# Attention on one Trainium2 core: PSUM shared out with four banks for scores and three in the ring of turned blocks

## The reference, cut to what matters

```python
s = jnp.einsum('bqgre,bige->bqgri', qg, kc) * SCALE          # scores
p_cmp, _ = _masked_softmax(s, mask)                          # mask, exp(s - max), divide by the sum
o_cmp = jnp.einsum('bqgri,bige->bqgre', p_cmp, vc)           # probabilities times values
...
o = g[..., 0:1] * o_cmp + g[..., 1:2] * o_slc + g[..., 2:3] * o_win
```

## Time and profile before

| | us |
|---|---|
| median of 3 runs | 1948.7 |
| lowest and highest run | 1945.65 and 1949.38 |
| profiled execution, its time | 1947.66 |
| profiled execution, its span | 1945.5 |
| TensorE busy in the span | 1826.0 (94%) |
| VectorE, ScalarE, GpSimd busy | 1041.1, 755.8, 264.0 |

### The profile page before, as it was taken

The page is one execution under the profiler, slowest core; times in us unless marked ns, Lnnn a source line. Parts: engine busy times, 40 slices in busy tenths (PEclk is TensorE's granted clock), DMA queues, the critical chain, the costliest instruction groups (busy, mean ns, idle before and its releaser), DMA issues. The chain is left out here.

```text
span 1945.5 us, 31487 instructions
## 1 busy us (share of the span) xinstructions
PE 1826.0 (94%) x12115; PEld 1539.0 (79%) x12115; DVE 1041.1 (54%) x2536; ACT 755.8 (39%) x1583; POOL 264.0 (14%) x344
## 2 busy tenths in 40 slices
PE   5999998988999889999987999999999999999998
PEld 4777787886777666666656889989989989989987
DVE  5978835335666566666654444344444444444444
ACT  4544433205777556655543233222212212213211
POOL 1000000003444344444430000000000000000000
PEclk8999999998999999999998999999999999999999
DMA  5233233515666322232236221212213113112202
GB/s 187 89 111 130 106 118 105 167 25 136 180 172 165 91 92 89 90 116 85 86 92 201 76 79 61 92 65 74 78 66 107 46 66 108 44 65 92 82 22 97
DMA packets 172107, 192.30 MB, mean 99 GB/s; under 512 B 55334, under 2 KB 138534, under 8 KB 169688
## 3 DMA queue, kind: packets, MB, share of 16 engines
q1 hardware_dynamic: 169618, 175.70, 28.9%
q0 software_dynamic: 2352, 14.73, 2.2%
HBM read 168.72 MB, written 59.81 MB: 117 GB/s over the span
## 5 line engine op out<-in xcount | busy, mean ns | idle before, releaser
L2274 PE MATMUL o_py<-f_h_hi,m_gu_hi 128*128 128x384 f32 (+1 forms) x1056 | 196.7, 328 | 0.5 <-DVE m_gu_lo L2458 0.5
L2274 PE MATMUL o_py<-f_h_lo,m_gu_hi 128*128 128x384 f32 (+1 forms) x1056 | 195.3, 327 | 0.0
L2274 PE MATMUL o_py<-f_h_hi,m_gu_lo 128*128 128x384 f32 (+1 forms) x1056 | 195.3, 327 | 0.0
L1847 DVE CUSTOM_DVE_ANT_0 l_e<-l_s,k_masks 128x1024 f32<-128x1024 f32 (+3 forms) x192 | 138.4, 721 | 103.9 <-PE l_s L1492 101.2
L2274 PEld LDWEIGHTS o_py<-f_h_hi,m_gu_hi 128*128 128x128 f32 x1056 | 176.8, 188 | 10.8 <-issue 8.1
L1792 ACT ACTIVATE l_e<-l_e,l_nmin 128x640 f32<-128x640 f32 (+11 forms) x224 | 169.0, 754 | 33.8 <-DVE l_nmin L1847 32.0
L2274 PEld LDWEIGHTS o_py<-f_h_lo,m_gu_hi 128*128 128x128 f32 x1056 | 176.9, 188 | 0.0
L2274 PEld LDWEIGHTS o_py<-f_h_hi,m_gu_lo 128*128 128x128 f32 x1056 | 176.9, 188 | 0.0
L2509 DVE SCALAR_TENSOR_TENSOR a_kv_nat<-m_ext,m_taps,a_kv_nat 128x384 f32<-128x384 f32 (+1 forms) x66 | 37.9, 574 | 170.5 <-ACT m_ext L2397 157.4
L2396 ACT ACTIVATE a_kv_nat<-o_py,m_taps 128x384 f32<-128x384 f32 (+1 forms) x33 | 21.6, 655 | 272.8 <-PE o_py L2274 272.8
L1532 PE MATMUL l_t<-k_ident,l_e 128*128 128x128 f32 x816 | 123.6, 276 | 0.2 <-DVE l_pT L1844 0.2
(11 more groups left out here) (305 smaller groups left out, 3642.5 us busy)
## 6 DMA issues: line engine op xcount, KB each, us to landing
m_raw_gu<-in_w_gate SPq DMA_DIRECT2D x22, 512.0 KB, 4.0
m_raw_gu<-in_w_up SPq DMA_DIRECT2D x22, 512.0 KB, 5.3
m_raw_d<-in_w_down SPq DMA_DIRECT2D x11, 1024.0 KB, 4.8
k_first<-in_w_in SPq DMA_DIRECT2D x5, 2048.0 KB, 8.2
a_kd_k<-in_state_dil SPq DMA_DIRECT2D x8, 1024.0 KB, 8.2
a_kd_v<-in_state_dil SPq DMA_DIRECT2D x8, 1024.0 KB, 7.9
a_kd_k<-in_cache_slc SPq DMA_DIRECT2D x128, 64.0 KB, 1.9
k_w<-in_w POOLq DMA_DIRECT2D x4, 1024.0 KB, 6.4
```

The source lines that it names most:

```text
L1847: return nc.vector.tensor_tensor_reduce(out=dst, in0=src, in1=m, scale=1.0, scalar=CLAMP, op0=ALU.add, op1=ALU.min, accum_out=low)
L2274: last = nc.tensor.matmul(bank[q % 2][:, 0:w], ws[k][:, m, c, :], hs[:, c, t0:t0 + w], start=(j == 0 and c == 0), stop=(j == 2 and c == KC ...
```

## The change

The number of score banks becomes a constant of four and the ring has three banks instead of four. The output bank stays. `score_banks` places every unit anew by the same rule over four banks.

```diff
-    used, at, prior = [-1, -1, -1], {}, {}
+    used, at, prior = [-1] * S_BANKS, {}, {}
     for u in range(NU):
         n = -(-width(u) // 512)
-        first = min(range(3 - n + 1), key=lambda x: (max(used[x:x + n]), x))
+        first = min(range(S_BANKS - n + 1), key=lambda x: (max(used[x:x + n]), x))
...
-RING = 4
+RING = 3
+S_BANKS = 4
...
-        s_all = ctx.enter_context(nc.psum_tensor("l_s", [P, 3 * 512], F32))
+        s_all = ctx.enter_context(nc.psum_tensor("l_s", [P, S_BANKS * 512], F32))
         S_AT, S_PRIOR = score_banks()
-        s_ps = lambda u: s_all[:, S_AT[u] * 512:min(S_AT[u] * 512 + 1024, 3 * 512)]
+        s_ps = lambda u: s_all[:, S_AT[u] * 512:min(S_AT[u] * 512 + 1024, S_BANKS * 512)]
```

## The result

The changed kernel takes 1951.8 us (median of 20 runs) against 1948.6 for the kernel before (median of 20): ratio 1.0018, 95% interval 1.0011 to 1.0024. It is 3.2 us slower. The direction was forecast and the time lies in the range, but the sum was +8.6 us, so more than half of it did not come. The profiled execution has a span of 1950.8 us, 5.3 more than that of before. Of these 1.3 us lie ahead of the attention part and some 1.1 behind it, where the change touches nothing; the attention part itself is 2.8 us longer.

What follows compares the result with a forecast made beforehand. TensorE was taken as the full engine: busy 189.0 of 198 us in the dilated passes, 339.6 of 379 in the sparse. 14.8 + 7.0 - 13.2 = +8.6 us on 1947.66 gave 1956, range 1949 to 1964.

Steps and rivals of the forecast that it cites:

- The dilated loss: Dilated passes: the shorter ring makes chunks wait for copies; 2.8 us an even pass, 0.9 an odd, 14.8 in all.
- The large stall: Before d6 in even dilated passes: the `kd` load waits for VectorE's copy behind d7's mask, 546.77 to 548.45; 1.1 us lost.
- The smaller stalls: Dilated passes: about 0.3 us each, 6 us in all; a rival (0.20) had them absorbed, giving about 1950.
- The last dilated pass: Its wait on the split of K (2.0 us) moves with TensorE's transposes; loss put at the mean, 1.85 us.
- The sparse loss: Sparse passes: ring waits at c (0.4 us) and w6 (0.3), 0.7 more in passes 10 and 11 each; 7.0 us together.
- The gain: Sparse passes: the fourth score bank removes score waits on masks at l4, w4 and l7; 13.2 us, bounds half to all.
- The first sparse pass: One more score wait, for masks brought by DMA; the next chunk waits for VectorE in that mask, so nothing gained.
- the rival of a faster kernel: Sparse passes: running ahead halves the 7.8 us wait for c's norm, smaller stalls cost nothing; 1943 to 1945, chance 0.08.
- The clock rival: Even dilated passes: each pause of up to 1.7 us lowers TensorE's clock; three add 5 us, 1961, chance 0.10.
- The signs: `l_nmin` waits under 2 us; new waits before `kd` and at K; dilated 12 to 17 us longer, sparse 4 to 8 less.
- the 0.2% that was given 0.22: Whole kernel: a time within 3.9 us of no change, chance 0.22; slower 0.70, faster 0.08.
- the 0.62 case: Whole kernel: the forecast itself, +4 to +13 us, 1952.5 to 1961, chance 0.62.

Runs made afterwards that it cites:

- three banks each: Three score banks and a ring of three, one PSUM bank unused, so the changed kernel without its fourth score bank: 1969.0 us, ratio 1.0105 to the kernel before.
- gates at l4 and w4: Changed kernel, but scores of l4 and w4 in sparse passes wait again for the mask of the unit just before: 1965.8 us.
- corrected dilated exchange: Changed kernel, with the engine emptying turned blocks in dilated passes chosen by place so that both long stalls fall to ScalarE: 1941.3 us.
- exchange of l6: Changed kernel, with the two chunks of sparse unit l6 exchanged: ScalarE empties the first, VectorE the second: 1944.5 us.
- both dilated exchanges: Two kernels, each the changed one with engines chosen by place in dilated passes: first try by one rule for all nine units, 1954.7 us; corrected rule, 1941.3 us.
- gate at l7: Changed kernel, but scores of l7 in passes 9 to 15 wait again for the mask of the unit before: 1953.5 us.
- both exchanges: Changed kernel with the engines exchanged both in the dilated passes (corrected rule) and for l6's two chunks in the sparse ones: 1937.7 us.
- both exchanges and a ring of four: Kernel before (three score banks, ring of four) with the engines exchanged in the dilated passes and for l6's chunks: 1946.6 us, ratio 0.9990.

## Why the prediction was right, and where it was off

The forecast of +8.6 us had two halves, +14.8 in the dilated passes and 7.0 - 13.2 = -6.2 in the sparse ones. Counted from pass to pass, the first took 13.9 us more (0.9 under) and the second 11.1 less (4.9 under). These two make the 5.8 us that the sum missed.

- **The dilated loss (14.8 us).** Right by its own steps. Even passes 3.0 us for 2.8, odd 0.8 to 1.1 for 0.9; the first 1.6 for 1.85. The large stall was placed to 0.1 us (1.65 us of idle loads against the shift of 1.68), and d6 came 1.05 us later for 1.1. What was read out as certain, that a copy behind a mask does not come earlier when TensorE pauses, held at these two large stalls in passes 2, 4 and 6. The smaller stalls are real too: the large ones make up 1.9 us of the 3.0.
- **The last dilated pass (1.85 us).** It took 0.4 us more, by luck. Up to the unit sd it had lost 1.5 us by the two stalls. The low clock of the earlier trace rows did not come in this execution, which gave 1.4 back.
- **The sparse loss (7.0 us).** Right at 0.7 us a pass in most passes, too high by 1.5 in all. The run with three banks each lost 5.5 us besides the low clock. The extra 0.7 us put on each of passes 10 and 11 "by the same size" came to 0.35 and nothing, and pass 8 lost only 0.2.
- **The gain (13.2 us).** This is the term that was mis-sized. "I take the whole idle time, 13.2 us" took it from matmul rows. The losses had been read from the starts of weight loads. A matmul's row runs on beyond the start of the next one, so its idle time misses that overlap. The rows below are the changed kernel's at l4 of pass 12. The transposes' row lasts until 866.11 and the first scores start at 865.87, 0.24 us before that; at the gate of the kernel before they started 0.51 us behind that row's end. 0.51 + 0.24 = 0.75 us, the idle time of the load. So the gate costs the idle time of the load, 2.15 us a pass and 17 us in all. The upper bound, "all of it", was thus no bound. This is 3.7 of the 5.8 us that the sum missed.

```profile
865.51 0.60 PE L1650 MATMUL l_t<-k_ident,a_kd_k 128*128 128x128 f32 x4
865.84 0.19 PEld L1492 LDWEIGHTS l_s<-l_kB,l_qT 128*128 128x128 f32 x1
865.87 0.48 PE L1492 MATMUL l_s<-l_kB,l_qT 128*128 128x512 f32 x1
```

- **The first sparse pass (nothing).** From the scores of l7 to those of c it took 6.1 us against 7.5. The rows below are VectorE's mask of l7, before and after. It waited 1.30 us for the DMA of the masks before, and not at all after. The run with three banks each shows nearly the same (6.25), so this is not the fourth bank's. VectorE waited so in all four kernels here with a ring of four, and in none of the eight with a ring of three. Why the masks landed in time there stays open. It is 1.3 us that the sum missed. The stretch of low clock in the same pass took 1.6 us back.

```profile
648.39 1.22 DVE L1847 CUSTOM_DVE_ANT_0 l_e<-l_s,k_masks 128x1024 f32<-128x1024 f32 x1 [1.30 <-DMA k_masks<-in_masks]
```

```profile
662.40 1.23 DVE L1848 CUSTOM_DVE_ANT_0 l_e<-l_s,k_masks 128x1024 f32<-128x1024 f32 x1
```

- **The rivals.** The smaller stalls were not absorbed. The waits for the norm of c did go, as the rival of a faster kernel had it, but waits of the ring (0.77 and 0.71 us in an even pass, last section) took their place, and the spot lost 0.5 us a pass. The clock rival came true once, and not where it was put: no pause of a dilated pass lowered the clock behind its start, but pass 8 has a low stretch, behind a wait of 1.1 us for the norm of c and one of 0.3 us for the ring. The kernel before waits 1.4 us at once for that norm and keeps its clock. The stretch cost 1.6 us (7.9 us between the scores of w6 and l1, against 6.3 in the kernel with gates at l4 and w4, which has none there), about what the missing one of the earlier trace rows gave back. That the two nearly cancel is luck.
- **The signs.** The waits on `l_nmin` went, the waits before `kd` (1.4 us) and at K after sd (0.7) came, and the dilated passes took 12.5 us longer, all as forecast. The sparse ones took 9.7 us less, outside the 4 to 8 that were named.
- **The chances.** The time lies 3.2 us up, inside the 0.2% that was given 0.22 and under the 0.62 case's +4 to +13. It got there not by that rival's way but by the larger gain. The range held it, with errors on both sides that partly cancel. Its upper end takes the clock rival or half the gain, not both: together they give 20 us, about 1969.

## What to carry to other kernels

Measure a wait by the idle time of the weight loads, on both sides of a trade, not by that of the matmuls: without the gate the first matmul would start before the row ahead of it ends. When buffers are taken from a ring, list for each chunk the one that it will now wait for and who empties that, in stage order and not in the order of the units; a chunk whose emptying engine must first do something long is the one to hand to the other engine. A trade of buffers that comes out even can hide two effects of 10 us, and the losing half may be cheap to repair: two exchanges of copies turned +3 us into -11, where the same two gave 2 to 3 us on the kernel before.

## What the hardware showed that I had not expected

The granted clock of TensorE falls in single stretches whose place changes between kernels that do nearly the same work there. In the kernel with gates at l4 and w4 it happened in pass 12, not in 13 (windows and timeline of that kernel):

```profile
857.31:860.72 3.41, 2.05 (x14) 1.28 (x13) 3.25 (x11) 2.68 (x6) 2.48 (x3) 1.00 0.26 77
860.72:864.14 3.42, 3.25 (x16) 1.85 (x18) 1.77 (x6) 1.81 (x6) 1.53 (x2) 0.50 0.57 153
```

```profile
858.82 0.55 PE L1535 MATMUL l_t<-k_ident,l_e 128*128 128x128 f32 x3 [0.77 <-DVE l_pT L1847]
...
860.89 1.06 PE L1541 MATMUL l_t<-k_ident,l_e 128*64 128x128 f32 x4 [0.71 <-DVE l_pT L1847]
861.88 3.04 PE L1582 MATMUL l_o<-l_pT,l_v 128*64 128x256 f32 x16
```

Two pauses of 0.8 and 0.7 us of the shorter ring stood close together, and behind them sixteen matmuls took 3.04 us instead of the 1.95 of the kernel before; the pass lost 1.5 us more than its neighbour. Two pauses stand at this spot in each of passes 9 to 15 of the changed kernel and lowered the clock in none of them. The second is 0.71 us there in the even passes and 0.46 in the odd ones, so passes 12 and 13 are not quite alike. Its one low stretch, in pass 8, lies at the same place in the pass, behind two unlike ones of 1.1 and 0.3 us. In the profiled execution of the corrected dilated exchange it happened at the same spot of two passes, 10 and 13 (windows):

```profile
758.72:762.13 3.41, 3.39 (x18) 2.41 (x20) 2.32 (x6) 1.66 (x6) 1.91 (x3) 0.50 0.59 154
895.25:898.66 3.41, 3.41 (x16) 1.94 (x18) 1.56 (x5) 1.59 (x6) 1.54 (x2) 0.50 0.25 53
```

All eleven low stretches in the sparse passes of the six kernels with a ring of three and without the exchange of l6 lie at this spot, between the scores of unit sc and those of l1: three in the kernel with gates at l4 and w4, two each in the one with three banks each and in both dilated exchanges, one each in the changed kernel and in the one with a gate at l7. In the two kernels where the second pause is gone there is none. The one with both exchanges (windows):

```profile
452.00:1007.00 555.00, 524.95 (x4496) 382.46 (x4495) 369.54 (x1173) 355.90 (x832) 235.92 (x304) 1.00 0.41 119
```

The shorter ring is not the only way to it. The kernel with both exchanges and a ring of four has one such stretch at this spot in pass 8, behind a wait of 1.85 us.

The Trainium skill (TensorE: Matmul & The Clock Gate, "A second HAM failure mode: psum-queue depth-cycling") tells of short idle times between groups of matmuls, as a kernel cycles through PSUM banks, that make the clock swing. These traces fit it, at 1.5 to 1.6 us a time, but no run takes the pauses alone away: the exchange of l6 changes other things too. Of the seven stretches in passes 9 to 15 six lie in even passes, behind the longer second pause, and one in pass 13, behind the shorter. What decides in which of them it happens stays open.
